# Squares of a gated norm made by token tile inside the scan, their parts added by GpSimd, one product of ones in place of eight

## The chip, the cores and the metric

The program runs on one core of a Trainium2 chip. The metric is the time of one execution on the device, in microseconds. A core has four compute engines with a queue of instructions each: TensorE (PE in the profile; PEld is its weight load), VectorE (DVE), ScalarE (ACT) and GpSimd (POOL). SyncE (SP) issues most of the loads of weights; GpSimd and ScalarE issue others. Engines wait for each other through semaphores, and each queue is worked off strictly in order.

## The reference

Two layers of a hybrid backbone over 128 context tokens and 256 latent tokens (384 in all, three tiles of 128), 1024 wide, in float32. The change is in the first layer's mixer, where the state-space heads are gated and normalised before they are joined with the Hyena channels:

```python
z, xbc, dt_raw, hy = jnp.split(proj, [...], axis=-1)
...
y, final = bidirectional_ssd(xs, dt_raw, Bm, Cm, A_log, dt_bias, init_state)
y = y + xs.astype(jnp.float32) * d_skip.astype(jnp.float32)[:, None]
y = rmsnorm(y * jax.nn.silu(z), g_ssd)       # y * rsqrt(mean(y*y) + eps) * g
parts = jnp.split(dwconv_centred(hy, hy_conv_w, hy_conv_b), 1 + HY_ORDER, axis=-1)
filters = hyena_filters(L, hy_w1, hy_b1, hy_w2, hy_b2, hy_w3, hy_freq)
```

The mean of `rmsnorm` runs over 1024 channels of each token. Later come the output projection, a mixture of experts, and the second layer with its own experts.

## The kernel before, in words

Everything is held with the channels on the partitions: `szT` is 128 partitions by 8 channel blocks by 384 tokens and holds first silu(z), then the gated product. `xtok` holds the scan's inputs by token instead, 128 tokens by 1024 channels for each of the three tiles.

The scan goes through twelve steps, `QUADS`: for each of the three token tiles `t` four groups `q` of four heads. In a step ScalarE makes ramps (`ramps`, L1892) and the exponential (L1936), GpSimd one product (`m2`, L2861), VectorE three products (`weigh`, L2368 and L2370; `decay_product`, L2393), TensorE the outputs; then VectorE adds the skip term (L2411, from PSUM) and multiplies into `szT` (L2414, from PSUM). Between the steps stand the terms of the entering states (`state_terms`, L2382 and L2386). TensorE also begins the first two chunks of the next projection, `hy (0,0)` and `hy (0,1)`, in the gaps of the scan.

When the last output has been multiplied in, ScalarE squares `szT` in eight blocks of 384 tokens into `sqssd` (L1943). TensorE finishes the two chunks, and then `sum_squares` multiplies a matrix of ones with each of the eight blocks, adding all in one bank: each partition then holds the sum over 1024 channels of every token. ScalarE takes the root (`root`, L1785) after the pads of chunks 0 and 1, VectorE the reciprocal (L2421), and `norm_product` (L2424) follows the convolution of each of chunks 0 to 7.

The projection `hy` has 24 chunks, `(q, c)` with q from 0 to 2 and c from 0 to 7, each eight products of 384 columns. ScalarE copies a chunk into `hpad` (`pad_chunk`, L1948 and L1949), VectorE convolves it (L2451 to L2455). After chunk `(0,2)` TensorE makes the first product of the filter network, `("f", 0)`, and waits before it for the semaphore `hyc_in` to reach 16 * 11, that is for eleven small loads. GpSimd issues these: after the last output of the scan it clears `hpad` (L2870) and `conds[1]` (L2871), whose areas the scan used, and then issues the eleven loads (L2873 to L2880) into areas that the scan used as well. ScalarE's first pads wait for the cleared `hpad`.

TensorE's queue is written out by hand in this order; the PSUM bank of each piece follows from the order of `bank_plan`. The weights come in blocks of 2 MB in a ring of six, each block's load waiting in SyncE's queue for TensorE's last use of the block before it (L790); the experts' weights are loaded the same way (L807 to L832).

Of the kernel before, what the change touches and what calls it, by code (L numbers as in the profile page):

```python
# [10 lines left out]
ALU = mybir.AluOpType  # L11
# [79 lines left out]
OUT_BANK = (6, 0, 1, 4, 5, 2, 3, 7)  # L91
FILTERS_AFTER = ("hy", 2, 5)
LAST_UTK, LAST_SPEC_S, LAST_INV = ("utk", *HYO[-1], 1), ("inv", *HYO[-1], 0, 0), ("inv", *HYO[-1], 1, 1)
assert len(FIRST) % NSLOT == 3 and len(SECOND) % NSLOT == 0 and 3 * PAIRS % NSLOT == 0
# [21 lines left out]
def bank_plan():  # L116
# [77 lines left out]
    for q in range(3):  # L194
        for c in range(KD):
            job(("hy", q, c), "act", ("hy", q, c // 4) if c % 4 == 3 else None, FILL_BANK[c] if (q, c) in ((0, 0), (0, 1)) else None)
            if (q, c) == (0, 1):
                job(("ss", "ssd"), "act")
            if ("hy", q, c) in F_AFTER:
                job(("f", F_AFTER[("hy", q, c)]), "dve")  # L200
            ada_after(("hy", q, c))
            if ("hy", q, c) == FILTERS_AFTER:
                for i, (s, x, t) in enumerate(HY_FILTERS):
                    job(("PQ", *HYO[0], s, x, t), "act", None, (7, 6, 1)[i % 3])
            if (q, c) == GATES_AFTER:
                job(("gr", 0), "act")
                job(("gr", 1), "act")
# [255 lines left out]
def build_kernel(nc, A, K, outs):  # L463

    with ExitStack() as ctx:
        sems = {}

        def S(name):
            if name not in sems:
                sems[name] = ctx.enter_context(nc.semaphore(name))  # L470
            return sems[name]
# [55 lines left out]
        grows = (area(18432, D), area(2 * D, D))  # L527
        sqssd = area(6144, KD, T)

# [132 lines left out]

        SQ_N = [("ssd", KD), ("q", 2), ("kv", 1)]

# [249 lines left out]
        def _(pe):  # L914
# [400 lines left out]
            for q in range(3):  # L1315
                for c in range(KD):
# [6 lines left out]
                    else:  # L1323
                        project(("hy", q, c), block_view(("hy", q, c // 4)), c % 4 * P, hT)
                    if (q, c) == (0, 1):
                        sum_squares("ssd", sqssd, KD)
                    if F_AFTER.get(("hy", q, c)) == 0:
# [315 lines left out]
            ps = open_bank("ckvtok")  # L1643
            pe.wait_ge(S("ckvn"), 1)
            tr(ps[:, 0:P], ckvT[:, 0:P])
            tr(ps[:, P:P + ROPE], krT[0:ROPE, 0:P]).then_inc(done, 1)
            took(pe, "mctx")
            pe.wait_ge(S("qn"), 2)
            pe.wait_ge(S("wmla_in"), 16 * 6)
# [110 lines left out]
        def _(act):  # L1760
# [157 lines left out]
            def take_state(d):  # L1918
# [7 lines left out]
                if d == 0:  # L1926
                    for i in range(2):
                        for g in range(2):
                            full(act, "sinit", i, g)
                            A_(sent[:, 3 * i, g * 512:(g + 1) * 512], bank("sinit", i, g)[:, :], ACT.Copy).then_inc(taken["act"], 1)  # L1930

            for n, (t, q) in enumerate(QUADS):
                full(act, "E", t, q)
                if n >= 2:
                    act.wait_ge(S("mm"), n - 1)
                A_(expEs[n % 2].rearrange("p h l -> p (h l)"), bank("E", t, q)[:, :], ACT.Exp).then_inc(taken["act"], 1)  # L1936
                if n + 2 < len(QUADS):
                    ramps(n + 2)
                if STATE_AFTER.get(n - 1, 2) < 2:
                    take_state(STATE_AFTER[n - 1])  # L1940
            took(act, "y", NT - 1, 3)
            for k in range(KD):
                A_(sqssd[:, k, :], szT[:, k, :], ACT.Square).then_inc(S("sq"), 1)  # L1943

# [8 lines left out]
            pad_chunk(1)  # L1953
            root("ssd", D)

# [7 lines left out]
            for c in range(3 * KD):  # L1963
                if c >= 2:
                    act.wait_ge(S("hconv"), c - 1)
                    pad_chunk(c)
                if ("hy", c // KD, c % KD) in F_AFTER:
                    i = F_AFTER[("hy", c // KD, c % KD)]
# [235 lines left out]
        def _(dve):  # L2204
# [214 lines left out]
            took(dve, "y", NT - 1, 3)  # L2419
            took(dve, "ss", "ssd")  # L2420
            link(nc.vector.reciprocal(rstd, rstd))  # L2421

            def norm_product(k):
                STT(out=szT[:, k, :], in0=szT[:, k, :], scalar=col("ssd_norm", k), in1=rstd, op0=mult, op1=mult).then_inc(S("yn"), 1)  # L2424

# [20 lines left out]
            for c in range(3 * KD):  # L2446
# [10 lines left out]
                last.then_inc(S("hconv"), 1)  # L2457
                if c < KD:
                    norm_product(c)
                if ("hy", q, k) in F_AFTER:  # L2460
# [327 lines left out]
            for k in range(2):  # L2788
                STT(out=latT[:, k, :], in0=latT[:, k, :], scalar=col("mla_q_norm", k), in1=rstd, op0=mult, op1=mult).then_inc(S("qn"), 1)
            took(dve, "ss", "kv")  # L2790
            link(nc.vector.reciprocal(rkv, rkv))
            STT(out=ckvT[:, 0:T], in0=latT[:, 2, :], scalar=col("mla_kv_norm", 0), in1=rkv, op0=mult, op1=mult).then_inc(S("ckvn"), 1)
            took(dve, "qr", 1)
# [29 lines left out]
        def _(pool):  # L2823
# [24 lines left out]
            def enter_state(d):  # L2848
# [5 lines left out]
                                        tot.unsqueeze(2).to_broadcast([P, HEADS, HDIM]), ALU.mult).then_inc(S("entering"), 1)  # L2854

            for n, (t, q) in enumerate(QUADS):
                hs = slice(4 * q, 4 * q + 4)
# [8 lines left out]
                if n in (1, 2):  # L2866
                    enter_state(n - 1)

            full(pool, "y", 2, 3)
            nc.gpsimd.memset(hpad, 0.0).then_inc(S("hpad0"), 1)  # L2870
# [203 lines left out]
```

## Time and profile before

| | us |
|---|---|
| median of three runs (1284.48 to 1286.18) | 1284.57 |
| span of the profiled execution, first to last instruction | 1282.6 |
| TensorE busy | 1204.8 (94%) |
| VectorE busy | 458.2 (36%) |
| ScalarE busy | 325.3 (25%) |
| GpSimd busy | 231.2 (18%) |

The profiled execution's own time is its span and what lies before the first and after the last instruction; the page gives the span alone, 2.0 us under the median of the runs. A busy TensorE is not TensorE at its peak, since ends of matmuls are modelled. A float32 product counts as two in the trace (x16 is eight products). The granted clock reads 1.00 at TensorE's upper level (2.4 GHz) and 0.50 at its lower (1.2 GHz); the page gives it in tenths, where 9 is 0.9 or more.

### The profile page before, as it was taken

The numbers are of one execution on the slowest core, as the hardware profiler recorded it, in microseconds if no ns is written. First come the engines' busy times: TensorE is split into PE (matmuls) and PEld (weight loads), VectorE is DVE, ScalarE is ACT, GpSimd is POOL, SyncE is SP. The second block draws the span as 40 slices with busy tenths as digits, with TensorE's granted clock in tenths as the row PEclk, the third lists the DMA queues.
The fourth block names the chain that finished last, engine by engine and source line by source line (L and its number), as shares of the span: only waits on it lengthen the run. The fifth ranks groups of instructions, "written<-read, shape, count | busy, mean of one in ns | idle before, by whom it ended". The sixth has DMA issues, their size and how long they took to land.

```text
span 1282.6 us, 16879 instructions
## 1 busy us (share of the span) xinstructions
PE 1204.8 (94%) x6504; PEld 678.7 (53%) x6504; DVE 458.2 (36%) x963; ACT 325.3 (25%) x831; POOL 231.2 (18%) x281
## 2 busy tenths in 40 slices
PE   6999999999999999999999878999999989999786
PEld 4455654555455554466555443755555575555442
DVE  1452088643237850162111112323374251111115
ACT  4313374301022300141111112414353331111113
POOL 1000053200033511011212111444010011212102
PEclk9999999999999999999999999999999999999998
DMA  9997910675940109439999998962330879999995
GB/s 341 359 387 262 367 60 1 224 270 200 375 131 1 66 10 416 142 136 406 419 419 419 419 420 355 369 97 39 139 111 1 334 280 420 418 420 420 421 420 207
DMA packets 94516, 343.15 MB, mean 268 GB/s; under 512 B 12734, under 2 KB 16532, under 8 KB 69617
## 3 DMA queue, kind: packets, MB, share of 16 engines
q1 hardware_dynamic: 73680, 309.47, 61.4%
q0 software_dynamic: 13872, 25.78, 7.4%
q10 hardware_dynamic: 6897, 6.97, 1.6%
q8 instruction: 47, 0.77, 0.2%
q14 instruction: 20, 0.16, 0.0%
HBM read 340.35 MB, written 28.43 MB: 288 GB/s over the span
## 4 chain that ended last, share of the span: by engine, by line
PE 74%; DMA 15%; DVE 5%; POOL 3%; ACT 2%; issue 2%; SPq 0%; DVEq 0%; ACTq 0%; POOLq 0%
PE bank L927 65%; DMA arena<-in_moe_w_down_dram 5%; PE bank L931 5%; DMA ring<-in_moe_w_down_dram 4%; DMA ring<-in_moe_w_up_dram 3%; PE bank L958 3%; DMA ring<-in_w_ada_dram 2%; PE bank L1706 1%; POOL ring L2905 1%; POOL hT L2908 1%; DVE arena L2727 1%; POOL arena L2908 1%; DMA arena<-in_hy_freq_dram 0%; PE bank L1012 0%; DVE arena L2724 0%
## 5 line engine op out<-in xcount | busy, mean ns | idle before, releaser
L927 PE MATMUL bank<-ring,arena 128*64 128x256 f32 (+3 forms) x2592 | 422.5, 429 | 34.5 <-DMA ring<-in_moe_w_up_dram 12.0
L927 PEld LDWEIGHTS bank<-ring,arena 128*64 128x64 f32 (+1 forms) x2592 | 212.8, 143 | 215.4 <-issue 109.5
L927 PE MATMUL bank<-hT,ring 128*128 128x384 f32 (+2 forms) x928 | 293.7, 472 | 1.0 <-DVE hT L2260 0.7
L927 PEld LDWEIGHTS bank<-hT,ring 128*128 128x128 f32 x928 | 170.4, 190 | 119.1 <-issue 16.2
L927 PE MATMUL bank<-arena 128*64 128x256 f32 (+7 forms) x858 | 130.9, 396 | 7.6 <-DMA arena<-in_moe_w_down_dram 1.7
L2683 DVE TENSOR_TENSOR hT<-hT,bank 128x256 f32<-128x256 f32 x32 | 13.5, 420 | 242.1 <-ACT hT L2047 242.1
L927 PEld LDWEIGHTS bank<-arena 128*64 128x64 f32 (+3 forms) x858 | 62.3, 143 | 58.9 <-issue 38.0
L2047 ACT ACTIVATE hT<-bank 128x256 f32<-128x256 f32 x32 | 12.3, 384 | 230.8 <-PE bank L927 230.8
L931 PEld LDWEIGHTS bank<-cst,hT 128*128 128x128 f32 x368 | 46.7, 190 | 38.2 <-issue 34.3
L2688 DVE COPY arena<-bank 128x512 f32<-128x512 f32 x32 | 22.1, 691 | 121.3 <-PE bank L927 101.5
L927 PE MATMUL bank<-ring,hT 128*128 128x512 f32 x144 | 63.0, 593 | 0.0
L931 PE MATMUL bank<-cst,hT 128*128 128x128 f32 x368 | 59.0, 294 | 2.5 <-DVE hT L2683 2.2
L2967 POOL COPY scr<-arena 128x1 int32 x28 | 5.1, 182 | 264.8 <-ACT arena L2058 156.4
L2058 ACT ACTIVATE arena<-bank 128x512 f32<-128x512 f32 x32 | 19.1, 597 | 113.2 <-PE bank L927 95.7
L927 PEld LDWEIGHTS bank<-ring,hT 128*128 128x128 f32 x144 | 27.0, 190 | 31.8 <-issue 31.7
L2950 POOL DMA_INDIRECT hT<-rows,scr x32 | 32.8, 1024 | 54.4 <-PE bank L931 23.1
L2451 DVE TENSOR_SCALAR arena<-arena,par 128x385 f32<-128x385 f32 x24 | 11.5, 481 | 82.9 <-ACT arena L1949 82.8
L927 PE MATMUL bank<-arena,ring 128*128 128x128 f32 (+2 forms) x256 | 38.3, 307 | 1.8 <-POOL ring L2905 1.3
L931 PE MATMUL bank<-cst,arena 128*128 128x128 f32 (+2 forms) x214 | 29.0, 274 | 11.3 <-DMA cst<-in_k_cst_dram 8.9
L2956 POOL DMA_INDIRECT expert_rows<-arena,scr x30 | 30.8, 1026 | 42.1 <-POOL scr L2967 24.2
L927 PEld LDWEIGHTS bank<-arena,ring 128*128 128x128 f32 x256 | 32.1, 192 | 11.3 <-POOL ring L2905 3.8
L927 PE MATMUL bank<-arena,cst 128*128 128x512 f32 (+2 forms) x76 | 35.1, 582 | 1.9 <-issue 1.6
(338 smaller groups left out, 1224.2 us busy)
## 6 DMA issues: line engine op xcount, KB each, us to landing
ring<-in_moe_w_up_dram SPq DMA_DIRECT2D x28, 2048.0 KB, 20.5
ring<-in_moe_w_down_dram SPq DMA_DIRECT2D x26, 2048.0 KB, 19.4
ring<-in_w_ada_dram SPq DMA_DIRECT2D x24, 2048.0 KB, 15.5
ring<-in_moe_w_gate_dram SPq DMA_DIRECT2D x24, 2048.0 KB, 21.7
ring<-in_ev_w_in_dram SPq DMA_DIRECT2D x10, 2048.0 KB, 12.8
arena<-in_moe_w_gate_dram SPq DMA_DIRECT2D x8, 2048.0 KB, 13.4
arena<-in_moe_w_down_dram SPq DMA_DIRECT2D x6, 2048.0 KB, 22.1
ring<-in_ev_w_out_dram SPq DMA_DIRECT2D x4, 2048.0 KB, 16.2
```

The costliest lines, as they stand in the source:

```text
L927: return nc.tensor.matmul(out, lhsT, rhs, start=start, stop=stop_, skip_group_check=True)
L931: return nc.tensor.transpose(out, in_, ident[0:n, 0:n])
L958: last = nc.tensor.matmul(ps[32 * g:32 * g + 32, :], conds[l][:, k, at:at + 32], w[:, k, :], start=b == first and k < 4, stop=(l, b) in AD ...
L1706: nc.tensor.matmul(ps[a][:, 0:nk], qrT[rp, r, q0:q0 + P], krT[rp, keys], start=False, stop=True, tile_position=(j * ROPE, 0), skip_group_c ...
L2058: A_(ob[:, 0:512], banks[5][:, :], ACT.Copy).then_inc(s["d_act"], 1)
L2683: TT(hid[:, b, :], sg[:, b, :], banks[2 + b][:, HID:2 * HID], mult).then_inc(s["hid"], 1)
L2688: COPY(ob[:, 512:1024], banks[6][:, :]).then_inc(s["d_dve"], 1)
L2727: TT(y, y, bank("gff", l, v, h), mult).then_inc(S("weighed"), 1)
L2905: nc.gpsimd.tensor_tensor(y1, y1, yadd[(3 * turn - 3 + i) % 2], ALU.add).then_inc(S("spec"), 1)
L2908: nc.gpsimd.tensor_tensor(at, at, decay[b][:, s + t, :], ALU.mult).then_inc(S("pq"), 1)
L2950: nc.gpsimd.indirect_dma_start(xs[:, b, :], None, rows_d[l], bass.IndirectOffsetOnAxis(ap=at, axis=0), bounds_check=T - 1, oob_is_err=False)\
L2956: nc.gpsimd.indirect_dma_start(outs_d[l], bass.IndirectOffsetOnAxis(ap=idxc[:, 2 + b:3 + b], axis=0), ob, None, bounds_check=2 * T - 1, oo ...
```

## The change

- The squares are made by token tile. After step 5 of the scan ScalarE squares tile 0 of `szT` (1024 values in each partition), after step 9 tile 1, after the last step tile 2. They are written over `xtok`, whose tile is no longer read by then.
- GpSimd adds the eight channel blocks of a tile: three adds of 512, 256 and 128 columns, each on the result of the one before (`add_squares`). It does so after its product of step 7 for tile 0, after that of step 11 for tile 1, and right after that for tile 2. The clearing of `hpad` and the eleven loads come behind.
- TensorE makes one product of ones with the 384 summed columns. It stands one chunk later, after `hy (0,2)` and not after `hy (0,1)`. The root and the norm products move back with it: the root behind the pads of chunk 2, the norm products behind the convolutions of chunks 3 to 10.
- In the second layer two semaphores become one (`latn`); the order there stays.

```diff
+SUM_AFTER = (0, 2)
+SQUARES_AT = {5: 0, 9: 1}
+ADDED_AT = {7: 0, 11: 1}
...
-            if (q, c) == (0, 1):
+            if (q, c) == SUM_AFTER:
                 job(("ss", "ssd"), "act")
...
-                    if (q, c) == (0, 1):
-                        sum_squares("ssd", sqssd, KD)
+                    if (q, c) == SUM_AFTER:
+                        ps = open_bank("ss", "ssd")
+                        pe.wait_ge(S("summed_squares"), 3 * NT)
+                        mm(ps[:, 0:T].rearrange("p (t n) -> p t n", t=NT), ones, xtok[:, :, 0:P], True, True).then_inc(done, 1)
...
+            def token_squares(t):
+
+                took(act, "y", t, 3)
+                act.wait_ge(S("xw"), min(t + 2, 4))
+                A_(xtok[:, t, :].rearrange("p (k n) -> p k n", k=KD), szT[:, :, cols(t)], ACT.Square).then_inc(S("sq"), 1)
+
             for n, (t, q) in enumerate(QUADS):
...
-            took(act, "y", NT - 1, 3)
-            for k in range(KD):
-                A_(sqssd[:, k, :], szT[:, k, :], ACT.Square).then_inc(S("sq"), 1)
+                if n in SQUARES_AT:
+                    token_squares(SQUARES_AT[n])
+            token_squares(NT - 1)
...
             pad_chunk(0)
             pad_chunk(1)
-            root("ssd", D)
...
                     pad_chunk(c)
+                if (c // KD, c % KD) == SUM_AFTER:
+                    root("ssd", D)
...
             took(dve, "y", NT - 1, 3)
-            took(dve, "ss", "ssd")
-            link(nc.vector.reciprocal(rstd, rstd))
 
             def norm_product(k):
+                if k == 0:
+                    took(dve, "ss", "ssd")
+                    link(nc.vector.reciprocal(rstd, rstd))
...
-                if c < KD:
-                    norm_product(c)
+                if 0 <= c - SUM_AFTER[1] - 1 < KD:
+                    norm_product(c - SUM_AFTER[1] - 1)
...
+            def add_squares(t):
+                pool.wait_ge(S("sq"), t + 1)
+                for i in range(3):
+                    m = 512 >> i
+                    nc.gpsimd.tensor_tensor(xtok[:, t, 0:m], xtok[:, t, 0:m], xtok[:, t, m:2 * m], ALU.add).then_inc(S("summed_squares"), 1)
+                    pool.wait_ge(S("summed_squares"), 3 * t + i + 1)
+
             for n, (t, q) in enumerate(QUADS):
...
+                if n in ADDED_AT:
+                    add_squares(ADDED_AT[n])
+
+            add_squares(NT - 1)
             full(pool, "y", 2, 3)
             nc.gpsimd.memset(hpad, 0.0).then_inc(S("hpad0"), 1)
```

How the instructions stand on GpSimd from step 4 of the scan to the first loads, before (the rows from `arena,scr` are the products `m2` of the steps, the memsets those of `hpad` and `conds[1]`):

```order
L2861 TENSOR_TENSOR arena<-arena,scr 128x512 x8
L2870 MEMSET arena 128x780
L2871 MEMSET arena 128x432
L2873 DMA arena<-in_k_dft_dram 128x2048
L2874 DMA arena<-in_hy_w_dram 33x64
```

And in the changed kernel (line numbers are its own):

```order
L2880 TENSOR_TENSOR arena<-arena,scr 128x512 x4
L2872 TENSOR_TENSOR arena<-arena 128x512
L2872 TENSOR_TENSOR arena<-arena 128x256
L2872 TENSOR_TENSOR arena<-arena 128x128
L2880 TENSOR_TENSOR arena<-arena,scr 128x512 x4
L2872 TENSOR_TENSOR arena<-arena 128x512
L2872 TENSOR_TENSOR arena<-arena 128x256
L2872 TENSOR_TENSOR arena<-arena 128x128
L2872 TENSOR_TENSOR arena<-arena 128x512
L2872 TENSOR_TENSOR arena<-arena 128x256
L2872 TENSOR_TENSOR arena<-arena 128x128
L2892 MEMSET arena 128x780
```

Three adds stand behind the eighth product of the scan and six behind the twelfth; the memset, and all loads after it, have moved behind these six.

On TensorE at the end of the scan, before (`hT,ring` are products of the projection `hy`, `arena,cst` those with ones, `arena 64x384` is the filter network's first):

```order
L927 MATMUL bank<-rstd,arena 64x128 x2
L927 MATMUL bank<-cst,ring 64x128 x2
L927 MATMUL bank<-hT,ring 128x384 x2
L927 MATMUL bank<-arena,cst 128x384 x8
L927 MATMUL bank<-hT,ring 128x384 x8
L927 MATMUL bank<-arena 64x384
L927 MATMUL bank<-hT,ring 128x384 x8
```

And in the changed kernel:

```order
L929 MATMUL bank<-rstd,arena 64x128 x2
L929 MATMUL bank<-cst,ring 64x128 x2
L929 MATMUL bank<-hT,ring 128x384 x10
L929 MATMUL bank<-arena,cst 128x384
L929 MATMUL bank<-arena 64x384
L929 MATMUL bank<-hT,ring 128x384 x8
```

The eight products of `hy (0,2)` have moved ahead of the sum, which is one product, and the filter product now stands right behind it.

## Rows read from the trace of the kernel before

**Rows 1.** The page: granted clock in 40 slices; shares of the last chain by engine.
```profile
PEclk9999999999999999999999999999999999999998
...
PE 74%; DMA 15%; DVE 5%; POOL 3%; ACT 2%; issue 2%; SPq 0%; DVEq 0%; ACTq 0%; POOLq 0%
```

**Rows 2.** The chain's pieces, 205 to 262 us: start, length, what.
```profile
224.94 1.11 PE bank L927 x16
...
226.10 0.75 POOL arena L2870
...
232.46 6.05 DMA arena<-in_hy_freq_dram
...
238.56 6.21 PE bank L927 x18
```

**Rows 3.** Timeline of TensorE: start, length, engine, line, what [idle before, releaser].
```profile
227.84 5.40 PE L927 MATMUL bank<-arena,cst 128*128 128x384 f32 x16 [0.32 <-ACT arena L1943]
233.08 5.32 PE L927 MATMUL bank<-hT,ring 128*128 128x384 f32 x16
238.56 0.86 PE L927 MATMUL bank<-arena 33*64 33x384 f32 x2 [0.16 <-DMA arena<-in_hy_freq_dram]
```

**Rows 4.** Timeline of VectorE and GpSimd at steps 7 and 11 of the scan.
```profile
202.24 1.55 POOL L2861 TENSOR_TENSOR arena<-arena,scr 128x512 f32<-128x512 f32 x1 [1.55 <-DVE arena L2370]
...
204.99 0.68 DVE L2368 TENSOR_TENSOR rstd<-arena,scr 128x512 f32<-128x512 f32 x1
...
221.09 1.55 POOL L2861 TENSOR_TENSOR arena<-arena,scr 128x512 f32<-128x512 f32 x1 [1.55 <-DVE arena L2370]
...
222.64 0.68 DVE L2368 TENSOR_TENSOR rstd<-arena,scr 128x512 f32<-128x512 f32 x1
...
223.36 0.69 DVE L2370 TENSOR_TENSOR rstd<-rstd,arena 128x512 f32<-128x512 f32 x1
...
224.15 0.69 DVE L2393 TENSOR_TENSOR rstd<-rstd,ring 128x512 f32<-128x512 f32 x1
...
226.72 0.42 DVE L2414 TENSOR_TENSOR arena<-arena,bank 128x256 f32<-128x256 f32 x1
```

**Rows 5.** ScalarE's groups by line and form: busy us, mean ns, idle before.
```profile
L1959 ACT ACTIVATE arena<-bank 128x512 f32<-128x512 f32 x16 | 9.6, 597 | 3.9 <-PE bank L927 3.9
...
L1948 ACT ACTIVATE arena<-bank 128x128 f32<-128x128 f32 x24 | 6.6, 274 | 108.2 <-PE bank L927 105.0 <-DVE arena L2455 3.2
```

**Rows 6.** Timeline of GpSimd and VectorE early in the scan, where both work.
```profile
166.71 1.04 POOL L2861 TENSOR_TENSOR arena<-arena,scr 128x512 f32<-128x512 f32 x1 [1.42 <-DVE arena L2370]
...
176.70 1.89 POOL L2845 TENSOR_TENSOR ring<-arena,scr 128x1024 f32<-128x1024 f32 x1
176.73 2.41 DVE L2368 TENSOR_TENSOR arena<-arena,scr 128x512 f32<-128x512 f32 x1
...
183.12 1.89 POOL L2845 TENSOR_TENSOR ring<-arena,scr 128x1024 f32<-128x1024 f32 x1
183.15 1.28 DVE L2355 TENSOR_TENSOR arena<-arena,bank 128x512 f32<-128x512 f32 x2
```

**Rows 7.** Stretch: its us; each engine's busy us (instructions); granted clock; DMA share; GB/s.
```profile
1274.00:1276.00 2.00, 0.00 (x0) 0.00 (x0) 1.90 (x5) 1.34 (x5) 0.89 (x1) 0.50 0.03 8
```

**Rows 8.** TensorE's timeline: the same form of warm-up product, twice.
```profile
9.11 8.07 PE L927 MATMUL bank<-cst 128*128 128x256 f32 x24
...
1032.74 3.62 PE L927 MATMUL bank<-cst 128*128 128x256 f32 x16
```

**Rows 9.** TensorE's waits over the span: us in total, times, longest.
```profile
PE bank L927 <- DMA ring<-in_moe_w_up_dram: 12.0, 10, 1.7
```

**Rows 10.** Waits of SyncE's queue over the span: us in total, times, longest.
```profile
SPq L832 <- PE bank L927: 334.5, 73, 18.1
```

**Rows 11.** Timeline of VectorE: the first operation of a chunk's convolution.
```profile
254.39 0.48 DVE L2451 TENSOR_SCALAR arena<-arena,par 128x385 f32<-128x385 f32 x1 [3.77 <-ACT arena L1949]
```

**Rows 12.** Time to landing of the 32 loads of `in_na_rel_bias`, issued by GpSimd.
```profile
DMA to landing us min/median/max: 4.2/4.5/5.0
```

More of the change, by code:

```diff
@@ L527, in build_kernel @@
         grows = (area(18432, D), area(2 * D, D))
-        sqssd = area(6144, KD, T)
         szT = area(0, KD, T)
@@ L660, in build_kernel @@
         last_w, last_pos, last_base = area(19552, 12), area(19564, 6), area(19570, 1)
-        SQ_N = [("ssd", KD), ("q", 2), ("kv", 1)]
+        SQ_N = [("ssd", NT), ("q", 2), ("kv", 1)]
         def sq_base(which):
@@ L1643, in _ @@
             ps = open_bank("ckvtok")
-            pe.wait_ge(S("ckvn"), 1)
+            pe.wait_ge(S("latn"), 3)
             tr(ps[:, 0:P], ckvT[:, 0:P])
@@ L1647, in _ @@
             took(pe, "mctx")
-            pe.wait_ge(S("qn"), 2)
+            pe.wait_ge(S("latn"), 2)
             pe.wait_ge(S("wmla_in"), 16 * 6)
@@ L2788, in _ @@
             for k in range(2):
-                STT(out=latT[:, k, :], in0=latT[:, k, :], scalar=col("mla_q_norm", k), in1=rstd, op0=mult, op1=mult).then_inc(S("qn"), 1)
+                STT(out=latT[:, k, :], in0=latT[:, k, :], scalar=col("mla_q_norm", k), in1=rstd, op0=mult, op1=mult).then_inc(S("latn"), 1)
             took(dve, "ss", "kv")
             link(nc.vector.reciprocal(rkv, rkv))
-            STT(out=ckvT[:, 0:T], in0=latT[:, 2, :], scalar=col("mla_kv_norm", 0), in1=rkv, op0=mult, op1=mult).then_inc(S("ckvn"), 1)
+            STT(out=ckvT[:, 0:T], in0=latT[:, 2, :], scalar=col("mla_kv_norm", 0), in1=rkv, op0=mult, op1=mult).then_inc(S("latn"), 1)
             took(dve, "qr", 1)
```

## The prediction, made before the changed kernel had run

> **What bounds the kernel now.** I read the chain of waits on the profile's page first. TensorE holds 74% of it [rows 1], so what counts is what stands in TensorE's queue and what it waits for. Then I read the same chain piece by piece around the end of the scan [rows 2]. There it leaves TensorE: from 226.10 it runs through GpSimd (two memsets and eleven loads issued one after another), then through the landing of the last load, issued at 232.46 and down 6.05 us later, and it comes back to TensorE at 238.56 with the product of 33 rows that opens the filter network. TensorE's own timeline says the same: its queue holds eight products of ones (227.84, 5.40 us), then the chunk `hy (0,2)` (233.08, 5.32 us), then that filter product, marked as waiting for `in_hy_freq` [rows 3]. So between 226 and 238.5 TensorE's 10.7 us of work fit just inside a GpSimd and DMA chain of 12.4 us. The work that the change takes away lies beside that chain, and the work it gives GpSimd lies on it.
>
> **The products of ones.** A product of 384 columns is two rows of the trace: 5.40 / 8 = 0.67 us [rows 3]. Seven of eight go: 4.7 us less on TensorE. Its queue would reach the filter product 4.7 us sooner. It gains nothing, because that product waits for the loads anyway. Worth 0; it would be -4.7 us if the loads were not late.
>
> **The sum on GpSimd, ahead of the loads.** In the new order GpSimd's last three adds stand before the memset of `hpad` and all eleven loads, and they wait for ScalarE's square of the last tile, which waits for VectorE's last product of the scan. Before, the memset began at 226.10 [rows 2]. Now:
> - VectorE's last product starts at 226.72 and takes 0.42: 227.14 [rows 4].
> - The square is 1024 wide, a width no row shows. ScalarE takes 0.274 us for 128 and 0.597 for 512, that is 0.84 ns a column; 1024 gives 1.03 [rows 5]. I take 1.05 (ends 0.9 and 1.4): 228.2.
> - The three adds are 512, 256 and 128 wide, each waiting for the one before. Where nothing of VectorE held it up GpSimd took 1.04 us for 512 and 1.89 for 1024 [rows 6], so 1.66 ns a column on 0.19: 1.04 + 0.61 + 0.40 = 2.05. VectorE is idle here, since its next work waits for `hpad`. For the four hand-overs I allow 0.1 each. End 230.7.
>
> The memset moves from 226.10 to 230.7, **4.6 us later** (ends 4.0 and 6.0), and every load and the landing move with it.
>
> **The adds inside the scan.** `xtok` tiles 0 and 1 are added after GpSimd's products 7 and 11. GpSimd has the time, but the adds read SBUF while VectorE does. In this trace such a meeting is not shared: with a GpSimd operation of 1.89 us running from 176.70, VectorE's product of two SBUF operands took 2.41 us, against 0.68 elsewhere; where one operand is in PSUM (L2355, 1.28 for two, beside a GpSimd operation begun 0.03 earlier) it kept its time [rows 6]. I lay the adds on the rows of before [rows 4]:
> - Step 7: GpSimd's product ends at 203.79, the 512 add at 204.85 beside PSUM work of VectorE. The 256 add meets L2368 at 204.99 and holds it 0.5 us; the 128 add then holds L2370 for 0.4. Together 0.9.
> - Step 11: the product ends at 222.64. L2368 starts there, the 512 add waits for it and then holds L2370 until 224.35 (+1.0); the 256 add holds L2393 until 225.65 (+0.5). The 128 add meets PSUM work only. Together 1.5.
>
> VectorE sets the pace here: TensorE's outputs at 224.94 start 0.1 us after L2393 (224.15 + 0.69) [rows 2, 4]. So **2.4 us** on the path (ends 0 and 3.0). ScalarE's squares of tiles 0 and 1 come after its ramps, in its waits for TensorE: 0 (at most 0.2).
>
> The Trainium skill ("SBUF — State Buffer", section "Who interferes with whom") gives the same pairing as an exclusive lock that the loser waits out; by plain medians (0.68, as if nothing met) this term would be 0, by the lock it is the 2.4. The 2.41 us row agrees with the lock.
>
> **The long wait and the clock.** TensorE now has after its outputs (end 226.05 + 2.4) only the last 1.3 us of the chunks begun ahead, eight products (5.3) and one (0.7): it is done near 235.9. The filter product can start at 238.56 + 2.4 + 4.6 = 245.6. TensorE is idle for some 9.7 us. The page's granted clock is in its upper tenth in every slice but the last [rows 1], and after the start no wait of TensorE for weights is over 1.7 us [rows 9]; in the stretch behind the program's last matmul it reads 0.50 [rows 7]. I expect it to fall to the lower level (1.2 GHz) here too. Coming back costs: the warm-up products at the kernel's start ran 24 rows in 8.07 us, the same form later 16 in 3.62 us, so 24 in 5.43 [rows 8]: **2.6 us** lost (ends 0 and 3.5). What follows the filter product is dense TensorE work on the path, so the loss is real.
>
> The Trainium skill ("TensorE: Matmul & The Clock Gate", section "Part 1: The HAM clock gate") calls the half clock the default that activity releases. By that rule the drop in a wait this long is certain; by the page's clock column at the start (upper tenth [rows 1] while the products ran slow) it would be nothing. The durations of those products agree with the rule, not the column.
>
> **What is late next, and what passes on.** The root moves from before chunk 2's pads to behind them, the reciprocal and norm products one to three chunks later; VectorE waits 3.77 us for a later chunk [rows 11], and `yn` is wanted only at the end of the stage: 0. After the filter product TensorE runs on. A delay there is lost only if something later waits for what TensorE does not set. The queue of the experts' loads stood 334.5 us in 73 waits, all for TensorE [rows 10], so the later weights are late by the same amount.
>
> **The sum.** 4.6 + 2.4 + 2.6 - 0 = +9.6 us. The profiled execution's span is 1282.6; the runs' median is 1284.57, 2.0 us more for what lies around the span. 1282.6 + 9.6 + 2.0 = **1294.2 us**.
>
> **Rivals.**
> 1. *The clock stays up*: 7.0 us alone, 1291.6. For it: no gap of before inside the kernel shows a fall. Against it: at the end 0.50 is read in the first stretch without a matmul. 8%.
> 2. *VectorE is not held in the scan* (the adds fall into its gaps, or its delay is taken up in the waits for TensorE): 4.6 + 2.6, 1291.8. For it: the meetings depend on tenths of a microsecond. 14%.
> 3. *The loads are issued or land slower still.* VectorE was idle while GpSimd issued them; now the convolution of chunks 0 to 2 runs then, with three tensor_scalars of 0.48 us [rows 11]. If each held the issue up, 1.4 us more: 1295.6. 8%. The Trainium skill ("SBUF — State Buffer", section "SBUF: two separate sides") says that such a VectorE operation keeps GpSimd from writing descriptors; no row of before shows both at once.
> 4. *The loads land sooner*: 4.5 us, as the bias loads did [rows 12], and not 6.05, since the 2 MB weight block is ahead of them now: 1.5 less, 1292.7. 6%.
> 5. *The other side: the delay is made up behind*, at one place. In the expert stages TensorE waits for weights now and then, 12.0 us in all for `moe_w_up` [rows 9]. Were those loads issued on their own time, a TensorE 9.6 us late would wait less for them: 1284.6, and with the 4.7 us of products gone from an unhindered queue at best 1279.9. It decides from the point where a load is released by anything but TensorE. The queue's waits [rows 10] speak against it. 4% for no change, 2% for faster.
>
> That the change does not do what it says is ruled out by the order: one product of ones stands behind ten of `hT,ring`, and the memsets behind nine adds.
>
> **Chances and range.** The forecast has 58%, rivals 1 to 5 the 42% above. All but the last are slower by over 0.2% (2.6 us, about what can be told from no change here): slower 94%, same 4%, faster 2%. Low end: no hold in the scan, 4.0 for the loads' shift, 1.0 of the clock: 1289.6. High end: 6.0 + 3.0 + 3.5 is 1297.1, and part of rival 3 makes it 1297.5.
>
> **What would show it.** TensorE's filter product near 245.6 with a wait of about 9 us on `in_hy_freq`; GpSimd's memset near 233.1 (230.7 + 2.4); three adds of 1.0, 0.6 and 0.4 us behind a square of about 1.05; L2370 or L2393 of VectorE at 1.2 to 1.7 us once each at steps 8 and 11; a granted clock of 0.50 behind the wait and the rows of `hy (0,3)` at first 0.65 us each instead of 0.33. I am wrong if the wait on `in_hy_freq` is under 3 us, if the memset is not later than 229, or if the distance from the filter product to the end is shorter than in before by more than a microsecond.

## The result, and the profile after

The changed kernel takes 1292.44 us (median of 4 runs, 1291.00 to 1294.24), the kernel before 1285.03 beside it (4 runs): a ratio of 1.0061, 95% interval 1.0048 to 1.0073. Ratios here and below are those on record, from runs in the chip's fast state alone, and the quotient of two medians can differ from them in the fourth decimal (1.0058 here). The changed kernel is slower by 7.4 to 7.9 us, by which median of before one takes. The forecast was 1294.2, its range 1289.6 to 1297.5. The profiled execution took 1292.67 us, with a span of 1290.9 (before: 1282.6).

The chain of waits of the changed kernel around the end of the scan, start, length, what (to be held against [rows 2]):

```profile
228.22 1.11 PE bank L929 x16
...
230.00 0.43 DVE arena L2425
...
230.46 1.07 ACT arena L1940
...
231.66 1.27 POOL arena L2872
...
233.00 0.72 POOL arena L2872
...
233.80 0.46 POOL arena L2872
...
234.31 0.75 POOL arena L2892
...
238.31 2.55 POOL arena L2902 x5
240.86 2.24 DMA arena<-in_hy_freq_dram
...
243.14 9.55 PE bank L929 x18
252.69 3.57 PE bank L960 x32
```

The chain runs as it was laid out: VectorE's last product, the square, three adds, the memset, the loads, the landing, the filter product. Two lengths differ from those of before. The landing takes 2.24 us where it took 6.05 [rows 2], and the eighteen products behind it take 9.55 where they took 6.21. Of the three loads of `in_hy_freq`, before and then changed:

```profile
DMA to landing us min/median/max: 5.9/6.1/6.8
...
DMA to landing us min/median/max: 2.2/2.2/2.9
```

TensorE's own timeline of the changed kernel, start, length, engine, line, what [idle before, releaser], against [rows 3]:

```profile
228.22 0.44 PE L929 MATMUL bank<-rstd,arena 128*64 128x128 f32 x4 [1.77 <-issue]
...
229.25 8.41 PE L929 MATMUL bank<-hT,ring 128*128 128x384 f32 x20
237.50 0.81 PE L929 MATMUL bank<-arena,cst 128*128 128x384 f32 x2
243.14 1.29 PE L929 MATMUL bank<-arena 33*64 33x384 f32 x2 [4.83 <-DMA arena<-in_hy_freq_dram]
244.35 8.34 PE L929 MATMUL bank<-hT,ring 128*128 128x384 f32 x16
```

One product of ones (237.50) stands where eight stood. TensorE then waits 4.83 us, and the chunk behind it, `hy (0,3)`, takes 8.34 us. In before this chunk was:

```profile
239.35 5.43 PE L927 MATMUL bank<-hT,ring 128*128 128x384 f32 x16
```

The stretches of the changed kernel give the clock (length; busy us of PE, PEld, DVE, ACT, POOL; granted clock; DMA share; GB/s):

```profile
226.00:230.00 4.00, 2.23 (x20) 1.41 (x19) 3.54 (x8) 0.00 (x0) 1.50 (x2) 0.97 0.01 4
230.00:234.00 4.00, 4.00 (x9) 2.09 (x8) 0.42 (x1) 1.06 (x1) 2.19 (x3) 0.60 0.86 286
...
238.00:242.00 4.00, 0.30 (x1) 0.00 (x0) 3.58 (x10) 3.53 (x5) 3.41 (x7) 1.00 0.55 216
242.00:244.00 2.00, 0.86 (x2) 0.19 (x2) 0.00 (x0) 0.00 (x0) 0.00 (x0) 0.86 0.01 0
244.00:246.00 2.00, 2.00 (x4) 1.04 (x4) 1.43 (x4) 0.00 (x0) 0.00 (x0) 0.50 0.00 0
246.00:250.00 4.00, 4.00 (x8) 2.15 (x7) 1.39 (x3) 0.52 (x1) 0.00 (x0) 0.50 0.00 0
```

The clock is at 0.50, its lower level of 1.2 GHz, from 244 to 250, with TensorE busy all the time; it is back at 1.00 in 251 to 252, so the end of the chunk runs at full rate again and the `ada` products behind it take the 3.64 us of before. It also dipped in 230 to 234, behind the gap of 1.77 us at the scan's end; there it cost nothing, since TensorE had a wait ahead of it.

VectorE and GpSimd of the changed kernel at steps 7 and 11, from their timeline, against [rows 4]:

```profile
205.47 3.36 POOL L2872 TENSOR_TENSOR arena<-arena 128x512 f32<-128x512 f32 x3
206.71 0.68 DVE L2379 TENSOR_TENSOR rstd<-arena,scr 128x512 f32<-128x512 f32 x1
207.42 1.10 DVE L2381 TENSOR_TENSOR rstd<-rstd,arena 128x512 f32<-128x512 f32 x1
208.63 0.76 DVE L2404 TENSOR_TENSOR rstd<-rstd,ring 128x512 f32<-128x512 f32 x1
...
224.32 3.25 POOL L2872 TENSOR_TENSOR arena<-arena 128x512 f32<-128x512 f32 x3
224.36 1.77 DVE L2379 TENSOR_TENSOR rstd<-arena,scr 128x512 f32<-128x512 f32 x1
226.16 1.10 DVE L2381 TENSOR_TENSOR rstd<-rstd,arena 128x512 f32<-128x512 f32 x1
227.37 0.76 DVE L2404 TENSOR_TENSOR rstd<-rstd,ring 128x512 f32<-128x512 f32 x1
```

At step 11 the first product begins 0.04 us behind the first add and takes 1.77 us instead of 0.68, the next 1.10 instead of 0.69. At step 7 VectorE's first product takes its 0.68 and only the second is held (1.10); GpSimd's adds take 3.36 us there, 2.59 behind the scan, where VectorE is idle. The Trainium skill ("SBUF — State Buffer", section "Who interferes with whom") calls this an exclusive lock that the loser waits out; the 1.77 us row agrees.

**Where the 8 us are.** Start of one instruction in both profiled executions, and what lies between:

| part | predicted | measured |
|---|---|---|
| start of the kernel, before 30 us | 0 | +1.71 |
| hold of VectorE at step 7 | +0.9 | +0.42, made up ahead of step 8 |
| hold at step 11 | +1.5 | +1.57 |
| memset later still (square, adds) | +4.6 | +4.93 |
| issue of the eleven loads | 0 | +0.19 |
| landing of the last load | 0 | -3.81 |
| filter product (238.56, now 243.14) | +7.0 | +4.58, of it 2.87 behind the start |
| the lower clock, up to the `ada` products | +2.6 | +3.33 |
| `ada` products (244.71, now 252.62) | +9.6 | +7.91, of it 6.20 behind the start |

From there the distance stays or grows a little: the last 16 products of 128x512 start at 1266.61, before at 1258.37, +8.24. No later wait gives the delay back.

To compare kernels without the start, I use the stage's own distance: from VectorE's third last product of the scan (222.30 in before) to the first `ada` products of 32 rows at the stage's end (346.81). It is 124.51 us in before and 130.71 in the changed kernel, +6.20.

### The profile page after: what moved, and what is told of

Its sections match the earlier page's. It is cut to its first block, busy times and chain, and to the rows that moved or that the text cites. A ratio compares the mean times of both kernels' runs of the same rounds, so it can differ in the third digit from the quotient of the medians.

```text
span 1290.9 us, 16860 instructions
## 1 busy us (share of the span) xinstructions
PE 1206.5 (93%) x6490; PEld 679.2 (53%) x6490; DVE 460.6 (36%) x963; ACT 326.7 (25%) x827; POOL 240.1 (19%) x290
## 4 chain that ended last, share of the span: by engine, by line
PE 74%; DMA 14%; DVE 5%; POOL 3%; ACT 2%; issue 2%; SPq 0%; DVEq 0%; ACTq 0%; POOLq 0%
PE bank L929 65%; DMA arena<-in_moe_w_down_dram 5%; PE bank L933 5%; DMA ring<-in_moe_w_down_dram 4%; DMA ring<-in_moe_w_up_dram 3%; PE bank L960 3%; DMA ring<-in_w_ada_dram 2%; PE bank L1710 1%; POOL ring L2927 1%; POOL hT L2930 1%; DVE arena L2739 1%; POOL arena L2930 1%; PE bank L1014 0%; DVE arena L2736 0%; POOL ring L2857 0%
## 5 line engine op out<-in xcount | busy, mean ns | idle before, releaser
L929 PE MATMUL bank<-hT,ring 128*128 128x384 f32 (+2 forms) x928 | 298.1, 478 | 1.1 <-DVE hT L2271 0.8
L2972 POOL DMA_INDIRECT hT<-rows,scr x32 | 32.8, 1024 | 53.4 <-PE bank L933 22.1
L933 PEld LDWEIGHTS bank<-cst,arena 128*128 128x128 f32 (+2 forms) x214 | 24.5, 142 | 23.7 <-issue 10.6
```

Source lines behind the costliest of these rows:

```text
L929: return nc.tensor.matmul(out, lhsT, rhs, start=start, stop=stop_, skip_group_check=True)
L933: return nc.tensor.transpose(out, in_, ident[0:n, 0:n])
L2972: nc.gpsimd.indirect_dma_start(xs[:, b, :], None, rows_d[l], bass.IndirectOffsetOnAxis(ap=at, axis=0), bounds_check=T - 1, oob_is_err=False)\
```

## The experiments

| kernel | ratio to before [95%] | stage distance, us | wait ahead of the filter product, us |
|---|---|---|---|
| before, one product of ones | one run | 126.27 | 1.68 (3.21 ahead of the product of ones) |
| changed, again | 1.0058 [1.0042, 1.0073] | 130.53 | 5.18 |
| idle products, 10 | 1.0044 [1.0028, 1.0061] | 129.09 | 2.23 |
| idle products, 14 | 1.0045 [1.0029, 1.0060] | 127.38 | 0.49 |
| loads before the last adds | 1.0052 [1.0035, 1.0068] | 128.63 | 1.40 (3.19 ahead of the product of ones) |
| adds of tile 1 late | 1.0050 [1.0032, 1.0067] | 129.68 | 6.99 |
| filter product one chunk later | 1.0011 [1.0000, 1.0022] | 123.77 | 1.43 |
| all three | 0.9983 [0.9974, 0.9992] | 120.32 | 0 (1.07 ahead of the product of ones) |
| all three, more room | 0.9975 [0.9965, 0.9984] | 119.21 | 0 |
| before, filter product later | 0.9994 [0.9985, 1.0003] | 124.08 | 0 |
| before, large load last | one run | 124.28 | 0 |
| before, longer program | 0.9998 [0.9988, 1.0007] | 124.55 | 0.20 |

**Before, with one product of ones.** Only the last of the eight is made, so seven eighths of the sum of squares are left out.

```diff
-                    last = mm(ps[:, 0:T], ones, src[:, k, :], k == 0, k == n - 1)
+                    if which != "ssd" or k == n - 1:
+                        last = mm(ps[:, 0:T], ones, src[:, k, :], which == "ssd" or k == 0, k == n - 1)
```

> The kernel before with only the last of the eight products of ones (seven of the eight parts of the sum are left out, so the experts' routing may differ, and this run is read at the filter product and not by its total time). Distance meant: from VectorE's last product of the scan (226.72 in the kernel before) to TensorE's filter product (238.56): 11.84 us in before, 13.14 in the changed kernel. Theory (GpSimd's loads set the filter product): the distance stays at 11.8 within 0.5, TensorE waits some 5.5 us there, and the granted clock falls behind the wait. Rival (TensorE's own queue sets it, and the removed products are a gain): the distance falls by 4.7 to 7.1.

TensorE's timeline of this kernel (1286.21 us in its one run):

```profile
231.76 0.88 PE L927 MATMUL bank<-arena,cst 128*128 128x384 f32 x2 [3.21 <-ACT arena L1944]
232.54 5.43 PE L927 MATMUL bank<-hT,ring 128*128 128x384 f32 x16
239.65 0.86 PE L927 MATMUL bank<-arena 33*64 33x384 f32 x2 [1.68 <-DMA arena<-in_hy_freq_dram]
240.43 7.12 PE L927 MATMUL bank<-hT,ring 128*128 128x384 f32 x16
```

The 4.7 us of products turned into waits of 3.21 and 1.68 (0.32 and 0.16 in before). The filter product came 11.90 us behind VectorE's last product, 11.84 in before. So the products were worth nothing there, as the prediction had it. Behind the first wait the clock stayed at 1.00 and the chunk took its 5.43 us. Behind the second it fell to 0.50 (241 to 244), the next chunk took 7.12 us, and the stage became 1.76 us longer than in before. So in this profile taking the products out cost time: they had kept TensorE at work.

**Before, with the large load last.** Not all eleven loads are small: `k_dft` is 1 MB. Here it is issued behind the other ten.

```diff
-                dma(dft, K["k_dft"]).then_inc(S("hyc_in"), 16)
                 dma(w1t[0:HY_FEAT, :], A["hy_w1"][0]).then_inc(S("hyc_in"), 16)
 ...
+                dma(dft, K["k_dft"]).then_inc(S("hyc_in"), 16)
```

> The kernel before with the 1 MB load of the transform matrices issued last of the eleven, not first. Theory A (the small loads landed late in before because they queued behind that load, which shared the DMA engines with a 2 MB block): the small loads land 2 to 3 us after their issue, the 1 MB load some 5 us after its own at 232, so all is down near 237 and TensorE's filter product does not wait (distance 11.7, set by TensorE). Theory B (a small load from GpSimd takes 6 us at this place, whatever is ahead): small loads at 6 us, the 1 MB load at 8 us, filter product at 240, 1.5 us later than in before.

The `in_hy_freq` loads landed in 4.1 to 5.0 us instead of 5.9 to 6.8, between the two theories, with the 2 MB weight block on its way (issued at 227.1, down 9.0 us later). So taking the large load out of their way gives about half of the 3.8 us that the changed kernel gained. That is not how the changed kernel gained them, though: there `k_dft` still stands ahead of them in the queue, issued 5.46 us before the last of them (5.27 in before). What is gone is the block, issued at 229.35 and down at 237.8, before the first of them was issued (238.80). `k_dft` itself then lands in 5.1 us, 8.1 in before, and the load issued while it was still on its way took 2.9. The filter product gained 0.2 us (11.61 for 11.84), and the run took 1283.85 us beside 1283.77 of before.

**The changed kernel, with idle products in the wait.** Ten, then fourteen products of constants into a bank that nobody reads are put ahead of the wait for the loads, to keep TensorE at work.

```diff
+                        ps = open_bank("f", 0)
+                        heat(ps, 10)
                         pe.wait_ge(S("hyc_in"), 16 * 11)
-                        ps = open_bank("f", 0)
```

> The changed kernel with ten idle products (256 columns each, 4.5 us) between the product of ones and the filter product, into a bank that is written anew. Theory (the wait costs twice, once by itself and once by the clock that falls behind it): the filter product starts where it did, the chunk behind it takes 5.4 us and not 8.3, the clock reads 1.00, and the kernel takes 3.3 us less than the changed one, some 1289. Rival (the slow chunk has another cause, or the clock falls anyway): no change, 1292.

> The changed kernel with fourteen idle products (6.3 us) before the filter product, where ten had left a wait of 2.2 us and a clock at 0.58 behind it. Theory (any wait of some 1.5 us or more at this place lets the clock fall, and the fall costs up to 3.3 us): with the wait at 0.5 us or less the clock stays at 1.00, the chunk behind takes 5.4 us, and the kernel takes 2 to 3 us less than the changed one. Rival (idle products do not hold the clock): the chunk takes 7 to 8 us again and the kernel is no faster than with ten.

With ten, a wait of 2.23 us was left, and the clock fell all the same: 0.58 in 246 to 250, the chunk 7.12 us. With fourteen, TensorE's timeline reads:

```profile
236.43 6.21 PE L929 MATMUL bank<-cst 128*128 128x256 f32 x28
243.12 0.85 PE L929 MATMUL bank<-arena 33*64 33x384 f32 x2 [0.49 <-DMA arena<-in_hy_freq_dram]
243.91 5.43 PE L929 MATMUL bank<-hT,ring 128*128 128x384 f32 x16
```

The filter product starts where it did (243.12 for 243.14), the chunk takes 5.43 us for 8.34, and the stage distance is 3.33 us shorter than in the first profile of the changed kernel (130.71), 3.15 shorter than in the profile taken beside it (130.53), whose filter product stood 0.3 us later. That is the price of the clock by itself. In run times it is 1290.37 for 1292.46; the intervals of the two ratios overlap, the four runs of each do not.

**The changed kernel, loads before the last adds.**

```diff
-            add_squares(NT - 1)
             nc.gpsimd.memset(hpad, 0.0).then_inc(S("hpad0"), 1)
 ...  (the eleven loads)
+            add_squares(NT - 1)
```

> The changed kernel with the adds of the last tile behind the eleven loads; memset and loads start with the scan's last output as in before. Theory (landing depends on what the DMA engines carry): the last load lands about 6 us after its issue again, the filter product stands 11.8 us behind VectorE's last product, 1.3 less than in the changed kernel; wait 3.5 us, clock still falls; 1291. Rival (landing stays at 2.2 us, the delay was GpSimd's alone): distance 8.1, hardly a wait, 1284.

TensorE's timeline:

```profile
239.69 0.88 PE L929 MATMUL bank<-arena,cst 128*128 128x384 f32 x2 [3.19 <-POOL arena L2872]
241.98 1.54 PE L929 MATMUL bank<-arena 33*64 33x384 f32 x2 [1.40 <-DMA arena<-in_hy_freq_dram]
243.44 7.70 PE L929 MATMUL bank<-hT,ring 128*128 128x384 f32 x16
```

The loads went out 5.0 us sooner after VectorE's last product (5.9 for 10.9), met the weight block again (down at 241.4) and landed in 5.6 to 6.5 us, `k_dft` in 8.0. So the short landing of the changed kernel goes with the block being through: with the loads back beside it, it is gone. The adds now came last, and the product of ones waited for them. From VectorE's last product to the filter product it was 11.44 us, 13.14 in the changed kernel: 1.7 won of the 5 that the shift had cost.

**The changed kernel, adds of tile 1 behind the scan.**

```diff
-ADDED_AT = {7: 0, 11: 1}
+ADDED_AT = {7: 0}
...
-            add_squares(NT - 1)
             full(pool, "y", 2, 3)
+            add_squares(1)
+            add_squares(NT - 1)
```

> The changed kernel with the adds of tile 1 behind the scan's last output and not behind step 11's product. Theory (an add on GpSimd holds VectorE's products of two SBUF operands for its whole length): VectorE's three products of step 11 take 0.69 each again and not 1.77, 1.10 and 0.76; the scan ends 1.6 us earlier; the last adds begin 0.5 later, as those of tile 1 are in their way; filter product 1.1 us earlier; 1291.3. Rival (VectorE's long products there come from something else): they stay, and the total grows by 2.6 us to 1295.

VectorE's three products of step 11 took 0.68 and 0.69 again, and from its product of step 9 to that of step 11 it took 4.43 us, as in before (4.42; changed kernel 5.98). So the hold of 1.55 us is the adds'. TensorE's gap of 1.77 us went with it (0.20), and the filter product stood 1.1 us earlier in the stage, as expected. The wait ahead of the filter product grew to 6.99.

**The filter product one chunk later,** in the changed kernel and in the kernel before.

```diff
-F_AFTER = {("hy", 0, 2): 0, ("hy", 0, 6): 1}
+F_AFTER = {("hy", 0, 3): 0, ("hy", 0, 6): 1}
```

> The changed kernel with the filter product one chunk later, behind hy (0,3). Theory (the whole slowdown hangs on that one wait): the loads are down before TensorE gets there, no wait and no fall of the clock behind it, so 4.8 + 3.3 us less than the changed kernel: 1284, and against before the 4.7 us of products less the scan's hold of 1.6 and a slow stretch of 1.8 at the scan's end: 1283. Rival (the time is lost in GpSimd's adds and VectorE's held products, and TensorE's wait only shows it): not under 1289.

> The kernel before with nothing but the filter product one chunk later. Theory (before stood 0.9 us for the loads): 0.9 us less than before, at the edge of what can be told; the rest of what the best version gains comes from the seven products. Rival (all of the best version's gain comes from moving the filter product): 2 us or more less than before.

In the changed kernel this takes back 6.9 us of stage distance: a chunk of 5.3 us stands in the wait, 1.43 us of it are left. At 1285.25 us it is a little above the theory's 1284 and far below the rival's 1289. The clock still fell (0.71 in 242 to 246), and the `ada` products took 5.34 us, not 3.64. In the kernel before the same edit wins nothing that can be told (0.9994), since TensorE had hardly waited there (0.16 [rows 3]). What the edit repairs is the change's damage.

**All three together.** First with the adds of tile 1 ahead of the loads and those of the last tile behind them, sum and filter product behind `hy (0,3)`. Then with all six adds ahead of the loads and the filter product behind `hy (0,4)`:

```diff
-F_AFTER = {("hy", 0, 2): 0, ("hy", 0, 6): 1}
-SUM_AFTER = (0, 2)
-ADDED_AT = {7: 0, 11: 1}
+F_AFTER = {("hy", 0, 4): 0, ("hy", 0, 6): 1}
+SUM_AFTER = (0, 3)
+ADDED_AT = {7: 0}
...
-            add_squares(NT - 1)
             full(pool, "y", 2, 3)
+            add_squares(1)
+            add_squares(NT - 1)
```

> Both the sum and the filter product stand behind hy (0,3); adds of tile 1 behind the scan's last output, then memsets and loads, then the adds of the last tile. Theory: TensorE meets no wait from the scan's end on, VectorE is not held at step 11, the clock stays: 4.7 us of products and the old wait of 0.9 are gained, 1285.0 - 5.6 = 1279.4. Rival (fewer dense products at the scan's end let the clock fall anyway, or a wait appears elsewhere): 1283 or more.

This took 1282.06 us, where the theory gave 1279.4 and the rival 1283 or more. The stage became 4.2 us shorter than in before, not 5.6: 1.07 us of wait were left ahead of the product of ones. TensorE's waits for its first weight blocks, 2.0 us in this profile and 0 in before, come on top (last section).

> All six adds of tiles 1 and 2 right behind the scan's last output, then memsets and loads; the sum behind hy (0,3), the filter product behind hy (0,4). Theory: the wait of 1.07 us for the adds of the last tile goes, no other comes: 1 us less than the version with the adds behind the loads, 1281, which is 3 to 4 under before. Rival (the gain of fewer products is used up elsewhere): same as that version, 1282, or slower by a fall of the clock.

TensorE's timeline of the second:

```profile
228.58 11.88 PE L929 MATMUL bank<-hT,ring 128*128 128x384 f32 x36
240.29 0.81 PE L929 MATMUL bank<-arena,cst 128*128 128x384 f32 x2
241.03 3.64 PE L960 MATMUL bank<-ring,arena 128*32 128x512 f32 x32
244.60 5.43 PE L929 MATMUL bank<-hT,ring 128*128 128x384 f32 x16
249.96 0.85 PE L929 MATMUL bank<-arena 33*64 33x384 f32 x2
```

No wait is left from 228 to 252, and the clock is 1.00 in all stretches. The version takes 1281.25 us (before beside it: 1284.63), 3.2 to 3.4 less than before, and it beats both kernels. Its stage distance is 4.87 us shorter than that of the kernel before with its filter product later (124.08), close to the 4.7 us of the seven products. The gain of the change is real once TensorE waits for nothing here.

**The changed kernel again.**

> The changed kernel as it is, on the same chip as the three kernels beside it, so that they can be set against it. Expected: 7 us over before, within 1.5; the small loads land in 2.2 to 3 us again, the wait for them is 4 to 5 us, the granted clock falls behind it.

The second profile has the same holds (1.77, 1.10, 0.76), the same landing (2.3 us), a wait just over the 4 to 5 us expected (5.18), and the same fall of the clock (0.64 in 246 to 250).

**Before, with a longer program.** Two semaphores of the latent norm are merged, one is new, and GpSimd gets nine small memsets late in the kernel.

```diff
+                if l == 0:
+                    for i in range(9):
+                        nc.gpsimd.memset(xs[:, 0, 0:2], 0.0).then_inc(S("summed_squares"), 1)
+                        pool.wait_ge(S("summed_squares"), i + 1)
                 nc.gpsimd.memset(xs, 0.0).then_inc(S("xs0"), 1)
```

> The kernel before, whose work up to the experts stays the same in the same order; only its text is brought nearer to the changed kernel's: two semaphores of the latent norm become one, one new semaphore is made, and GpSimd gets nine memsets of two columns with a wait behind each, far behind, ahead of the clearing of the first expert rows (about 2 us of GpSimd where it waits for TensorE or clears). It asks whether the 1.5 to 2.9 us that every kernel derived from the changed one waits for its first weight blocks (0 to 0.8 in those derived from the kernel before) comes from the program's make-up. Theory A (it comes from the make-up: the number of GpSimd instructions or the semaphores' numbers): TensorE's waits before 160 us sum to 1.5 to 2.9 us, GpSimd's first loads take 7 to 8.5% of the DMA engines in the first 28 us, and the median is about 1.5 to 2.5 us above before's, and up to 2 us more where the nine memsets delay the gather. Theory B (it comes from something else of the change, as the tiles' addresses or the work itself): waits of 0 to 0.8 us, 3.3 to 4.8% of the DMA engines, and the stage's distance of before (124.5 us); the median within 1 us of before's, or up to 2 us above it by the memsets alone.

The time is that of before (0.9998). The waits for the first weight blocks sum to 1.4 us and GpSimd's first loads take 5.5% of the DMA engines, both between what the two theories gave. The theory that the program's make-up costs 1.5 us or more fell; whether it does a part of it, this one profile doesn't tell.

## Why the prediction was right, and where its sum was not

**Products of ones at 0: right for the filter product, not for the clock.** Leaving them out moved the filter product by 0.06 us (11.90 for 11.84), and with all waits taken away the stage was 4.87 us shorter than in the kernel before with its filter product later. But without them the wait opened behind which the clock fell: in before that made the stage 1.76 us longer (one profile). In the changed kernel 4.7 of the 4.83 us of wait are their place (an estimate, seven times the 0.67 us of [rows 3]), and idle products put there took back 3.33 us. The prediction counted the clock, but not as the price of this term.

**The hold of VectorE: right at step 11, not on the path at step 7.** At step 11, 1.57 us for the 1.5 laid out; undoing those adds gave it back. Which products were held was laid out wrongly, so the closeness is partly luck: the add came 0.04 us ahead of L2368, which was to go unhindered, and held it by 1.09, then L2370 by 0.41 and L2393 by 0.07, for 0, 1.0 and 0.5 (L2379, L2381 and L2404 of the changed kernel). At step 7 it was 0.42, not 0.9. The working had let every meeting go against VectorE; there it was GpSimd that lost the first one (VectorE's first product took its 0.68, the three adds 3.36 us, 2.59 without company). Ahead of step 8 the 0.42 was made up: VectorE waited there for TensorE, 0.74 us in before and 0.26 now, a slack that the prediction did not look for. Rival 2 (no hold) fell for one of the two steps.

**The shift of the loads: right.** 4.93 us for 4.6. The square took 1.06 for 1.05. The adds were slower, 1.27, 0.72 and 0.46 for 1.04, 0.61 and 0.40.

**The landing: the step that failed.** The sum kept 6.05 us for it. It took 2.24. With the start's 1.71 taken off, the filter product stood at 241.4, not 245.6: 3.8 of these 4.2 us are the landing, 0.9 the hold at step 7, and 0.6 go the other way. The wait was 4.83 us, not 9.7, since TensorE's queue also ended 0.7 us later than laid out, its chunk slowed by the fall of the clock at the scan's end. Rival 4 had seen the direction, since the weight block would be ahead of the loads, but took 4.5 us from the bias loads [rows 12]. The kernel with the loads before the last adds shows that the direction was seen rightly: beside the block they took 5.6 again. A delayed load is not a load with the same landing at a later time: it meets other traffic.

**The clock: right in kind, short in size.** 3.33 us for 2.6; the same by the idle products. The lower clock held for the filter product and a good half of the chunk, to about 250.3. Rival 1 (the clock stays up) fell. The Trainium skill ("TensorE: Matmul & The Clock Gate", section "Part 1: The HAM clock gate") has the half clock as the state that TensorE is in unless activity releases it; the traces agree here, the clock came back while TensorE worked.

**What passes on: right.** +7.91 at the `ada` products, +8.24 at the end. Rival 5 fell. Rival 3 fell as well: the eleven issues took 0.19 us more, not 1.4, though VectorE ran its tensor_scalars beside them. The Trainium skill ("SBUF — State Buffer", section "SBUF: two separate sides") ties the blocking of descriptors to VectorE's modes that use two ports; no row here tells whether these tensor_scalars ran in one, so the trace shows only that they cost next to nothing.

**The total.** The stage adds 6.2 us where 9.6 were forecast: 3.8 too much for the landing and 0.9 for step 7, 0.7 too little for the clock and 0.6 for hold, adds and issue. The median came only 1.8 us under the forecast because something outside the stage, which the sum did not have, adds to it (last section): that part is luck. So the number was nearer than its working.

## What to carry to other kernels

When loads are issued later, don't keep their landing time: ask what will be in their queue and on the DMA engines at the new time. Work taken from the bounding engine is worth nothing until the wait behind it is moved too; here one constant (the place of the filter product) turned a ratio of 1.006 into 1.0011, and with the adds moved too it came to 0.9975. Count a wait of the bounding engine twice, once for itself and once for the clock behind it: 4.83 us of wait cost 3.3 more, 1.68 us cost 1.7 more. And work that fills a wait keeps the clock up: taking it out is not free.

## What the runs showed of the hardware

**Small loads.** The same 0.2 KB loads of `in_hy_freq` landed in 5.9 to 6.8 us with a 1 MB load ahead in their queue and a 2 MB block of another queue both on their way (5.6 to 6.5 with the loads before the last adds), in 4.1 to 5.0 with the block alone, in 2.9 with the 1 MB load alone, and in 2.2 at or behind its end (changed kernel). With more room, the last of the three was issued at 240.64, just behind SyncE's next 2 MB block (240.49), and took 5.5 us, where the two before it took 2.8 and 2.3.

**The clock behind short waits.** At this place the granted clock fell behind waits, or before their end, of 1.40 (with one of 3.19 just before), 1.43, 1.68 (with one of 3.21 before), 2.23, 4.83, 5.18 and 6.99 us. It did not fall behind 0.49 and 1.07, and behind that wait of 3.21 it read 1.00 until the wait of 1.68 was over. Behind the gap of 1.77 us at the scan's end it fell in the two profiles of the changed kernel (0.60 in 230 to 234, 0.64 in 234 to 238) and stayed at 1.00 in four others with the same gap. So at this length it isn't settled by the program alone.

**A difference at the start, its cause open.** TensorE's timeline of the changed kernel around its first weights:

```profile
18.72 1.92 PE L1014 MATMUL bank<-ring,arena 128*32 128x512 f32 x16 [0.53 <-DMA ring<-in_w_ada_dram]
...
24.05 1.92 PE L1014 MATMUL bank<-ring,arena 128*32 128x512 f32 x16 [1.20 <-DMA ring<-in_w_ada_dram]
```

In before these start at 17.70 and 22.35 without such a wait. Nothing of the change stands there. GpSimd's first loads, the same 192 packets and 0.13 MB, take 8.2% of the DMA engines in the first 28 us, 3.9% in before, and the weights' queue moves 8.24 MB there instead of 8.68. The same holds for all nine profiles of kernels with the changed code: waits of 1.5 to 2.9 us for these blocks and 7.3 to 8.9% of the DMA engines. The four profiles with the code of before and its program about as long have 0 to 0.8 us and 3.3 to 4.8%. It fits that run times lie 1 to 2 us above what the stage distances give: the changed kernel +7.4 to +7.9 for +6.2, the best version -3.2 to -3.4 for -5.3. Nine more instructions of GpSimd and other semaphores did not bring it about in time. What does is open.
